# Eight modulation steps of the opening attention, and twelve of the first gather, cut into quarters and spread

## The chip, the cores and the metric

The kernel runs on one core of one Trainium2 chip. The metric is device time in microseconds (us) for one execution of the whole kernel; lower is better. Everything is in float32.

## The reference

Two transformer blocks with a shared residual stream `x` of 256 tokens by 1024 features. The first block has two layers with a second stream `ctx` of 256 tokens beside `x`; the second block has one layer. What matters here is the modulation: a small vector times a large matrix, whose six parts scale, shift and gate everything else.

```python
def _modulation(cvec, w_mod, b_mod):            # w_mod: 1024 x 6144 for each layer
    m = jax.nn.silu(cvec) @ w_mod + b_mod
    return jnp.split(m[:, None, :], 6, axis=-1)

for l in range(DEPTH):                           # DEPTH = 2
    m_x = _modulation(c, w_mod[l], b_mod[l])
    m_c = _modulation(c_ctx[None, :], w_mod[l], b_mod[l])
    h = _modulate(x, norm1_g[l], m_x[0], m_x[1])
    hc = _modulate(ctx, norm1_g[l], m_c[0], m_c[1])
    ...                                          # keys and values of ctx, attention, Fourier and pool branches
    x = x + m_x[2] * mix_x
    h2 = _modulate(x, norm2_g[l], m_x[3], m_x[4])
    x = x + m_x[5] * _peer(h2, w_pq[l], peer_keys[l], peer_down[l], peer_up[l])
```

`_peer` looks up, for each token, 128 rows of `peer_down` and 128 rows of `peer_up` (4 KB each), and is what most of the time goes to. The attention has 8 heads, 256 queries (two tiles of 128) and, in the part at hand, 512 keys.

## The kernel before

Each engine (TensorE, VectorE, ScalarE, GpSimd, SyncE) runs the same script, `main`, with its own subclass of `Walk`. A stage is a Python generator. Each `yield` ends a step, and the same step numbers hold on all five engines, since every subclass yields equally often. `self.run` plays one stage; `weave(front, back, rate, ...)` plays two at once: at every step of the front stage `rate` is added to an account, and while the account is at 1 or more a unit of the back stage is played and its cost (1.0, or what `at` says) is taken off. So the order on each engine's in-order queue is fixed when the program is built, by `rate`, by the costs and by the number of yields. Engines meet at semaphores, among them `full` and `free` of the eight PSUM banks (TensorE has written, the reader is done) and `w0` to `w2` (a weight buffer of 2 MB has landed).

The modulation of a layer is 12 steps j of `modvec`. One step is: SyncE loads a bias row and a 2 MB block of `w_mod` into a weight buffer; TensorE multiplies 8 times (2 columns by 512, the vector's columns stationary) into a bank; VectorE adds the bias; ScalarE stores 2 x 512 values to DRAM. SyncE starts a load into a buffer only when TensorE is through with what was in it (`fetch` waits for the mark `("w", ...)`, which the last of the eight products sets).

Two places use it inside a weave:

- The **beginning**. Steps 0 to 3 of layer 0 run by themselves. Steps 4 to 11 are the back stage of a weave whose front is `start1`: input projection (`tok_major`, 8 yields), queries, keys and values of the four token tiles (`qkv`, 6 + 6 + 3 + 3 yields), then `attend` (82 yields). The back has weight buffer 2 alone (slot "third"), the front buffers 0 and 1.
- The **first gather**, `weave(self.gather([0, 1, 2, 3], ...), ctx_then_x(queries), RATE0)` with 512 + 18 front steps, one for each looked-up row of a tile: GpSimd fetches a `peer_down` row and a `peer_up` row for each of 128 tokens, VectorE multiplies the former, TensorE sums the latter. `x_mix` plays the 12 steps of layer 1 in it, with buffers 0 and 1 by turns (slots "two").

In `attend` each head has two scores products (96 x 256), a maximum on VectorE, an exponential on ScalarE, four transposes on TensorE, a copy by VectorE (even heads) or ScalarE (odd heads), and four value products that wait for the copy. A head's values and the scores of the head two further on stand next to each other on TensorE.

Of the kernel before, what the change touches and what calls it, by code (L numbers as in the profile page):

```python
# [132 lines left out]
class Walk:  # L133
# [157 lines left out]
        pass  # L291

    def modvec(self, l, at, js):
        yield from self.units_of(len(js))

    def modsum(self, at, vectors):
        yield from self.units_of(4 * len(vectors) + 2)
# [126 lines left out]
    def main(self):  # L424

        K, A, NB = self.K, self.K.A, self.K.NB
# [6 lines left out]
        def temps(mem):  # L433
            return dict(qt=mem(768), kt=mem(768), kvt=mem(1024), junk=mem(256), rt=mem(3, 128), CQ=mem(2, 128), CK=mem(128))
# [7 lines left out]
        def att_bufs(mem):  # L442
            return [mem(512) for _ in range(2)], [mem(512) for _ in range(2)], mem(512)
# [6 lines left out]
        T0 = BG + 9216  # L450
# [10 lines left out]
        def mix_rest(l, who, HT, HP):  # L461
            self.small_weights(l)
            yield from self.at(1.0, self.spread(l, PL, FT, zpair(who), QT.rearrange("p (f c) n -> p f c n", c=2)[:, 0:2, :, :], QT[0:64, 4:8, :]))
            self.fence()
            mem = area((T0, NB))
            yield from self.at(1.5, self.gates(l, {0: AT, 1: FT, 2: PL}, QT, [mem(256) for _ in range(3)], mem(256), HT))
            self.fence()
            yield from self.at(3.4, self.project(l, who, QT, area((T0, NB))(512)))
            self.fence()
            yield from self.at(1.5, self.modulate(l, A["norm2_g"][l], 3, who, HP))  # L470
            self.fence()

        def start1():
            self.affine(K.arena[:, T0:T0 + 64], 0, HTx)
            self.affine(K.arena[:, T0:T0 + 64], 1, HTc)
            self.fence()
            for c0, n in ((0, 512), (512, 416)):
                yield from self.tok_major(0, c0, n, lambda i: K.H2[:, i, c0:c0 + n], (HTx, HTc))
            self.fence()
            self.small_weights(0)  # L480
            tm = temps(area((T0, NB)))
            for t in range(4):
                yield from self.qkv(0, t, zrow(t), tm, QT if t < 2 else None, (KTx, KTc)[t // 2], (VVx, VVc)[t // 2])
            self.small_done()
            self.fence()
            yield from self.attend(4, att_bufs(area((T0, NB))), QT, [(KTx, VVx), (KTc, VVc)], AT)
            self.fence()
# [22 lines left out]
        L1E = T0 + 4096  # L510

        def x_mix():
            yield from self.at(3.5, self.modvec(1, T0, range(12)))
            yield ("after", 2 * NEXT + LAG + 2)
            self.folded(2)
            self.fence()
            yield from self.at(1.5, self.modulate(1, A["norm1_g"][1], 0, 0, HTc))
            self.fence()
            for c0, n in ((0, 512), (512, 416)):
                yield from self.at(1.8, self.tok_major(1, c0, n, lambda i: K.H2[:, i, c0:c0 + n], (HTc,)))  # L520
            self.fence()
            self.small_weights(1)
            tm = temps(area((T0, NB)))
            for t in (0, 1):
                yield from self.at(1.4, self.qkv(1, t, zrow(t), tm, QT, KTc, VVc))
            self.fence()
            yield from self.spread(1, PL, FT, zpair(0), MX.rearrange("p (f c) n -> p f c n", c=2)[:, 0:2, :, :], MX[0:64, 4:8, :])
            self.fence()
            mem = area((L1E, NB))
            yield from self.at(1.6, self.gates(1, {1: FT, 2: PL}, MX, [mem(256) for _ in range(3)] + [ga], mem(256), HTc))  # L530

        def ctx_then_x(queries):
            yield from ctx_mix(queries)
            yield from x_mix()
# [14 lines left out]
        self.run(cols(2))  # L549
        self.run(cols(3))  # L550
        self.tables_there()
        self.weave(start1(), self.modvec(0, NB - 2048, range(4, 12)), 0.13, slots=("two", "third"))
        self.run(mix_rest(0, 0, HTx, HTp))
        self.slot, self.ring = self.slots["two"], self.rings["back"]
        queries = self.at(query_costs(3.2, 1.2, 0.7, 0.5), self.peer_q(0, 0, pt, HTp, QA))
# [1 line left out]
        self.weave(self.gather([0, 1, 2, 3], tables, gelu, [(0, 0, 5), (0, 0, 5), (0, 1, 5), (0, 1, 5)]),  # L557
                   ctx_then_x(queries), RATE0, done=done)
        self.folded(4)
# [142 lines left out]
class Vector(Walk):  # L702
# [76 lines left out]
    def modvec(self, l, at, js):  # L779
        K, S = self.K, self.S  # L780
        m = 2 if l < 2 else 1
        for j in js:
            bias, md = K.arena[0:m, at + 512 * (j % 2):at + 512 * (j % 2) + 512], K.arena[0:m, at + 1024 + 512 * (j % 2):at + 1536 + 512 * (j % 2)]
            b = self.bank()
            self.wait_ge(*self.full(b))
            self.wait_ge(*self.next(S.bias_in[j % 2], 16))
            stored = self.got.get(S.mod_out[j % 2].name, 0)
            if stored:
                self.wait_ge(S.mod_out[j % 2], stored)
            self.got[S.mod_out[j % 2].name] = stored + 16  # L790
            self.tt(md, b.ap[0:m, :], bias, AD, inc=self.drain(b))
            self.mark(("bias", l, j))
            yield
# [659 lines left out]
class Tensor(Walk):  # L1453
# [22 lines left out]
    def modvec(self, l, at, js):  # L1476
        K = self.K
        m, c0 = (2, 0) if l < 2 else (1, 2)
        for j in js:
            s = self.load()  # L1480
            w = s.ap.rearrange("p (k n) -> p k n", n=512)
            b = self.bank()
            self.wait_ge(*s.at)
            self.wait_ge(*self.vacant(b))
            for k in range(8):
                i = self.mm(b.ap[0:m, :], K.svb[:, k, c0:c0 + m], w[:, k, :], k == 0, k == 7)
            i.then_inc(*self.fill(b))
            self.rows_of[j] = b
            self.mark(("w", s.i, s.n))
            yield  # L1490
# [626 lines left out]
class Scalar(Walk):  # L2117
# [63 lines left out]
    def modvec(self, l, at, js):  # L2181
        K, S = self.K, self.S
        m = 2 if l < 2 else 1
        for j in js:
            md = K.arena[0:m, at + 1024 + 512 * (j % 2):at + 1536 + 512 * (j % 2)]
            b = self.bank()
            self.wait_ge(*self.drained(b))
            latest = self.latest
            self.e.dma_start(K.modd[2 * l:2 * l + m, 512 * j:512 * j + 512], md).then_inc(*self.inc(S.mod_out[j % 2], 16))
            self.latest = latest  # L2190
            yield
# [461 lines left out]
class Sync(Walk):  # L2653
# [17 lines left out]
    def modvec(self, l, at, js):  # L2671
        K, A, S = self.K, self.K.A, self.S
        m = 2 if l < 2 else 1
        src = A["w_mod"][l] if l < 2 else A["ada_w_2"][0]
        biases = A["b_mod"][l:l + 1, :] if l < 2 else A["ada_b_2"][0:1, :]
        if l:
            self.settled()
        for j in js:
            cs = slice(512 * j, 512 * j + 512)
            if j > 1:  # L2680
                self.wait_ge(*K.marks["bias", l, j - 2])
            self.e.dma_start(K.arena[0:m, at + 512 * (j % 2):at + 512 * (j % 2) + 512],
                             biases[0, cs].partition_broadcast(m)).then_inc(S.bias_in[j % 2], 16)
            self.fetch(self.load(), lambda a: a.rearrange("p (k n) -> p k n", n=512), src[:, cs].rearrange("(p k) n -> p k n", k=8))
            yield

    def tok_major(self, l, c0, n, dst, HTs):
        self.block(self.K.A["w_in"][l], c0, n)
# [80 lines left out]
        self.wait_ge(S.out, 32)  # L2769


RATE0 = 1.15
RATE1 = lambda s: 0.9 if s < 64 else 0.7 if s < 146 else 0.25
RATE2 = lambda s: 0.9 if s < 64 else 0.6
# [206 lines left out]
```

## Time and profile before

| | |
|---|---|
| median of 3 runs | 5015.89 us (5010.78 to 5027.59) |
| profiled execution | 5005.38 us, its span 5003.3 us |
| TensorE busy | 3628.7 us, 73% of the span |
| VectorE, GpSimd, ScalarE busy | 55%, 40%, 16% |
| DMA | 1328 MB, mean 265 GB/s |
| granted TensorE clock, mean | 0.807 of full speed |

The span is the time on the core from the first to the last instruction of the trace; the execution's own time is 2.1 us more. A TensorE product in float32 shows as two records, so eight products are "x16". The granted clock has two levels, 0.50 (1.2 GHz) and 1.00 (2.4 GHz); a value between is a stretch that had both.

### The profile page before, as it was taken

Reading aid. Unit: us, or ns where it says so; the run is one execution under the profiler, and the core shown is the slowest. Engines: PE = TensorE matmul, PEld = TensorE weight load, DVE = VectorE, ACT = ScalarE, POOL = GpSimd, SP = SyncE. Lnnn points to the kernel's source line nnn. Section 1 sums busy time; section 2 is a strip of 40 time slices with the busy share of each in tenths; the row PEclk is TensorE's granted clock in tenths of the full one; section 3 lists DMA queues with packets and bytes.
Section 4 is the critical chain, followed back from the end, with each engine's and each line's share of the span. In section 5 each row is a group of like instructions: output and inputs, shape, how many; then the busy total and the mean of one; then the engine's idle time right before and its main releaser. Section 6 shows DMA issues by size and latency. Waiting matters only on the chain.

```text
span 5003.3 us, 34906 instructions
## 1 busy us (share of the span) xinstructions
PE 3628.7 (73%) x10422; PEld 1830.2 (37%) x10422; DVE 2729.6 (55%) x5717; ACT 807.4 (16%) x1935; POOL 1992.1 (40%) x2088
## 2 busy tenths in 40 slices
PE   7679487877686676776564875676788886677776
PEld 3247343454342113541343421221366653332211
DVE  1211567454789646556545674576442222677676
ACT  1110112211121112111101111111121100111111
POOL 0000266554566543545102675475000000576775
PEclk9779799998776697986677998766778986899756
DMA  4234599999999998999436999898200002899999
GB/s 165 85 95 133 209 363 340 350 344 326 351 386 360 342 396 275 341 326 349 164 118 231 351 406 376 327 404 315 105 1 1 1 1 84 304 378 363 406 405 344
DMA packets 482032, 1328.11 MB, mean 265 GB/s; under 512 B 40396, under 2 KB 139980, under 8 KB 481336
## 3 DMA queue, kind: packets, MB, share of 16 engines
q0 software_dynamic: 301824, 1099.07, 57.9%
q1 hardware_dynamic: 173872, 204.09, 12.4%
q10 hardware_dynamic: 6152, 22.74, 1.3%
q8 instruction: 86, 1.41, 0.1%
q14 instruction: 98, 0.80, 0.0%
HBM read 1324.58 MB, written 1.17 MB: 265 GB/s over the span
## 4 chain that ended last, share of the span: by engine, by line
PE 24%; DMA 19%; DVE 8%; POOL 6%; issue 5%; ACT 2%; SPq 1%; ACTq 0%; DVEq 0%; POOLq 0%
PE ps L1458 23%; DMA arena<-in_peer_up,arena 7%; POOL arena L2649 6%; DMA arena<-in_peer_v,arena 4%; DVE arena L707 3%; DVE arena L720 3%; DMA arena<-in_w_mod 2%; ACT arena L2122 1%; DMA arena<-in_peer_down,arena 1%; DMA arena<-in_ada_w 1%; DMA arena<-in_peer_u,arena 1%; SPq L2661 1%; DMA arena<-in_w_oc 1%; PE ps L1464 1%; DMA arena<-mod_scratch 1%
## 5 line engine op out<-in xcount | busy, mean ns | idle before, releaser
L1458 PE MATMUL ps<-arena 128*128 128x512 f32 (+9 forms) x9844 | 3518.9, 511 | 1086.5 <-DMA arena<-in_peer_up,arena 330.7
L1458 PEld LDWEIGHTS ps<-arena 128*128 128x128 f32 (+4 forms) x9844 | 1739.3, 206 | 2808.5 <-issue 1382.6
L720 DVE SCALAR_TENSOR_TENSOR arena<-arena,ps 128x1024 f32<-128x1024 f32 x1024 | 1242.8, 1216 | 458.0 <-DMA arena<-in_peer_down,arena 284.0
L2649 POOL DMA_INDIRECT arena<-in_peer_down,arena x768 | 741.6, 966 | 1242.1 <-DVE arena L724 674.8
L2649 POOL DMA_INDIRECT arena<-in_peer_up,arena x768 | 735.0, 957 | 534.9 <-PE ps L1458 354.8
L2122 ACT ACTIVATE arena<-arena 128x128 f32<-128x128 f32 (+5 forms) x1250 | 446.9, 385 | 2152.2 <-PE ps L1458 975.2
L2649 POOL DMA_INDIRECT arena<-in_peer_u,arena x256 | 246.9, 964 | 896.5 <-DVE arena L724 804.1
L720 DVE SCALAR_TENSOR_TENSOR ps<-arena,ps 128x512 f32<-128x512 f32 x635 | 477.4, 752 | 121.3 <-DMA arena<-in_peer_up,arena 85.4
L707 DVE TENSOR_TENSOR arena<-ps,arena 128x512 f32<-128x512 f32 (+3 forms) x198 | 135.4, 684 | 563.8 <-PE ps L1458 533.2
L2122 ACT ACTIVATE arena<-ps 128x512 f32<-128x512 f32 (+3 forms) x345 | 175.1, 508 | 1198.9 <-PE ps L1458 885.9
L1464 PE MATMUL ps<-arena 128*128 128x128 f32 (+2 forms) x578 | 129.8, 372 | 282.0 <-DVE arena L707 194.9
L707 DVE TENSOR_TENSOR arena<-arena,ps 128x256 f32<-128x256 f32 (+2 forms) x136 | 74.4, 547 | 453.7 <-PE ps L1458 443.9
L2649 POOL DMA_INDIRECT arena<-in_peer_v,arena x256 | 243.8, 952 | 125.9 <-PE ps L1458 83.6
L707 DVE TENSOR_TENSOR arena<-arena 128x512 f32<-128x512 f32 (+9 forms) x412 | 252.1, 612 | 57.1 <-ACT arena L2122 38.6
L1464 PEld LDWEIGHTS ps<-arena 128*128 128x128 f32 (+2 forms) x578 | 94.2, 186 | 357.8 <-issue 183.3
L2122 ACT ACTIVATE arena<-ps,arena 128x256 f32<-128x256 f32 (+2 forms) x140 | 71.2, 509 | 712.7 <-PE ps L1458 441.6
L720 DVE SCALAR_TENSOR_TENSOR arena<-arena 128x512 f32<-128x512 f32 (+6 forms) x151 | 110.0, 729 | 63.2 <-DMA arena<-mod_scratch 56.1
L2122 ACT ACT_TABLE_LOAD x86 | 110.3, 1283 | 119.1 <-DVE arena L715 61.6
L724 DVE COPY arena<-ps 128x512 f32<-128x512 f32 (+5 forms) x69 | 39.6, 575 | 144.9 <-PE ps L1458 137.9
L728 DVE TENSOR_REDUCE arena<-ps 128x1 f32<-128x512 f32 (+2 forms) x50 | 30.3, 606 | 105.2 <-PE ps L1458 104.2
L1066 DVE MAX8 arena<-ps 128x8 f32<-128x128 f32 x128 | 28.7, 286 | 107.4 <-PE ps L1458 105.6
L720 DVE DVE_READ_ACCUMULATOR arena<-arena,ps 128x1 f32 x1024 | 83.6, 82 | 0.0
(33 smaller groups left out, 506.0 us busy)
## 6 DMA issues: line engine op xcount, KB each, us to landing
arena<-in_w_mod SPq DMA_DIRECT2D x24, 2048.0 KB, 13.5
arena<-in_w_in SPq DMA_DIRECT2D x72, 512.0 KB, 11.1
arena<-in_w_in SPq DMA_DIRECT2D x14, 2048.0 KB, 15.4
arena<-in_w_pq SPq DMA_DIRECT2D x12, 2048.0 KB, 10.0
arena<-in_ada_w POOLq DMA_DIRECT2D x24, 1024.0 KB, 7.4
arena<-in_w_out SPq DMA_DIRECT2D x8, 2048.0 KB, 11.4
arena<-mod_scratch ACTq DMA_DIRECT2D x26, 512.0 KB, 7.2
arena<-in_peer_down,arena POOLq DMA_INDIRECT x768, 6.9
```

The lines of the kernel that those rows point to most:

```text
L707: self.e.tensor_tensor(o, a, b, op).then_inc(*(inc or self.inc(self.S.vec)))
L720: self.e.scalar_tensor_tensor(o, a, s, b, op0, op1, accum_out=accum).then_inc(*(inc or self.inc(self.S.vec)))
L724: self.e.tensor_copy(o, a).then_inc(*(inc or self.inc(self.S.vec)))
L728: self.e.tensor_reduce(o, a, AX, op).then_inc(*(inc or self.inc(self.S.vec)))
L1066: e.max(v[j][:, 0:8], src[j]).then_inc(*self.inc(S.vec))
L1458: return self.e.matmul(o, l, r, start=start, stop=stop)
L1464: ins = self.e.transpose(o, x, self.K.ident)
L2122: self.e.activation(o, i, f, bias=bias, scale=scale, accum_out=accum).then_inc(*(inc or self.inc(self.S.act)))
L2649: self.e.indirect_dma_start(out=o, out_offset=None, in_=table, in_offset=bass.IndirectOffsetOnAxis(ap=idx.bitcast(U32), axis=0)).then_inc( ...
L2661: self.e.dma_start(f(s.ap), src).then_inc(self.S.w[s.i], 16)
```

## The change

`modvec` takes four yields for each j instead of one on every engine: TensorE issues two of its eight products in each, VectorE and ScalarE do their part in the fourth, SyncE issues the load in the first. In the beginning the rate 0.13 becomes 0.1 for the first 26 front steps and 0.45 after them; in the gather the cost 3.5 of a unit becomes 0.9.

```diff
     def modvec(self, l, at, js):
-        yield from self.units_of(len(js))
+        yield from self.units_of(4 * len(js))
...
         def x_mix():
-            yield from self.at(3.5, self.modvec(1, T0, range(12)))
+            yield from self.at(0.9, self.modvec(1, T0, range(12)))
...
-        self.weave(start1(), self.modvec(0, NB - 2048, range(4, 12)), 0.13, slots=("two", "third"))
+        self.weave(start1(), self.modvec(0, NB - 2048, range(4, 12)), lambda s: 0.1 if s < FIRST else 0.45, slots=("two", "third"))
...
             b = self.bank()
+            yield from self.units_of(3)
             self.wait_ge(*self.full(b))
...
             for k in range(8):
                 i = self.mm(b.ap[0:m, :], K.svb[:, k, c0:c0 + m], w[:, k, :], k == 0, k == 7)
+                if k % 2 == 1 and k < 7:
+                    yield
             i.then_inc(*self.fill(b))
...
             b = self.bank()
+            yield from self.units_of(3)
             self.wait_ge(*self.drained(b))
...
             self.fetch(self.load(), lambda a: a.rearrange("p (k n) -> p k n", n=512), src[:, cs].rearrange("(p k) n -> p k n", k=8))
-            yield
+            yield from self.units_of(4)
...
+FIRST = 26
```

By these numbers the units of the weave in the beginning stood behind front steps 8, 16, 24 (one each for j = 4, 5, 6) and 31, 39, 47, 54, 62 (j = 7 to 11). Now quarters of j = 4 stand behind steps 11, 21, 27 and 29, and the other 28 quarters two or three front steps apart from step 31 to step 91. The attention is steps 27 to 108.

TensorE's queue at the first heads of the attention, before. `2x512` is a product of `modvec`, `128x256` a scores product, `128x128` a transpose, `128x64` a value product; `w2` is the landing of the weight buffer.

```order
L1458 MATMUL ps<-arena 128x256 [waits free1]
L1458 MATMUL ps<-arena 128x256
L1458 MATMUL ps<-arena 2x512 [waits free7,w2]
L1458 MATMUL ps<-arena 2x512 x7
L1464 MATMUL ps<-arena 128x128 [waits free2,free0]
L1464 MATMUL ps<-arena 128x128 x3
L1458 MATMUL ps<-arena 128x64 [waits free2]
L1458 MATMUL ps<-arena 128x64 x3
L1458 MATMUL ps<-arena 128x256 x2
L1464 MATMUL ps<-arena 128x128 [waits free1]
L1464 MATMUL ps<-arena 128x128 x3
L1458 MATMUL ps<-arena 2x512 [waits free4,w2]
```

The same place now (all lines of the kernel behind line 781 have moved on by one or more):

```order
L1459 MATMUL ps<-arena 2x512 x4
L1459 MATMUL ps<-arena 128x256 [waits free1]
L1459 MATMUL ps<-arena 128x256
L1459 MATMUL ps<-arena 2x512 [waits w2]
L1459 MATMUL ps<-arena 2x512
L1465 MATMUL ps<-arena 128x128 [waits free2,free0]
L1465 MATMUL ps<-arena 128x128 x3
L1459 MATMUL ps<-arena 2x512 x2
L1459 MATMUL ps<-arena 128x64 [waits free2]
L1459 MATMUL ps<-arena 128x64 x3
L1459 MATMUL ps<-arena 128x256 x2
L1459 MATMUL ps<-arena 2x512 x2
```

The last four products of j = 4 and the first two of j = 5 now have one head's scores products between them, where a whole step had a head's work and more before the next; and a pair of products stands between a head's transposes and its value products.

TensorE's queue in the first gather, before. `128x512` with `up_in` is the sum of one looked-up row.

```order
L1458 MATMUL ps<-arena 2x512 [waits free5,w0]
L1458 MATMUL ps<-arena 2x512 x7
L1458 MATMUL ps<-arena 128x512 [waits up_in2,diagonal]
L1458 MATMUL ps<-arena 128x512 [waits up_in3,diagonal]
L1458 MATMUL ps<-arena 128x512 [waits up_in0,diagonal]
L1458 MATMUL ps<-arena 2x512 [waits free6,w1]
L1458 MATMUL ps<-arena 2x512 x7
```

And now:

```order
L1459 MATMUL ps<-arena 2x512 [waits free5,w0]
L1459 MATMUL ps<-arena 2x512
L1459 MATMUL ps<-arena 128x512 [waits up_in2,diagonal]
L1459 MATMUL ps<-arena 2x512 x2
L1459 MATMUL ps<-arena 128x512 [waits up_in3,diagonal]
L1459 MATMUL ps<-arena 2x512 x4
L1459 MATMUL ps<-arena 128x512 [waits up_in0,diagonal]
L1459 MATMUL ps<-arena 2x512 [waits free6,w1]
```

The eight products that stood in one block have a looked-up row's product between the pairs, and the number of rows for each modulation step is still three.

## Rows read from the trace of the kernel before

**Rows 1.** The page: the span, and DMA's busy tenths in 40 equal slices.

```profile
span 5003.3 us, 34906 instructions
...
DMA  4234599999999998999436999898200002899999
```

**Rows 2.** Stretches: length, TensorE busy (records), granted clock, DMA share, GB/s.

```profile
157.80:187.60 29.80, 20.00 (x47) 0.73 0.21 71
...
300.00:350.50 50.50, 39.35 (x136) 0.50 0.24 58
...
212.30:350.50 138.20, 103.97 (x344) 0.72 0.35 106
```

**Rows 3.** Timeline before the attention: start, us busy, what, [idle before, released by].

```profile
133.36 0.68 DVE L707 TENSOR_TENSOR arena<-ps,arena 2x512 f32<-2x512 f32 x1 [11.98 <-PE ps L1458]
...
136.57 0.66 PE L1464 MATMUL ps<-arena 128*128 128x128 f32 x2 [3.25 <-DVE arena L713]
...
146.59 1.94 PE L1464 MATMUL ps<-arena 128*96 128x128 f32 x8 [2.61 <-DVE arena L707]
...
157.84 0.69 PE L1464 MATMUL ps<-arena 128*128 128x128 f32 x2 [2.23 <-DVE arena L713]
...
187.60 0.48 PE L1464 MATMUL ps<-arena 128*128 128x128 f32 x1 [2.06 <-DVE arena L713]
...
197.90 0.48 PE L1464 MATMUL ps<-arena 128*128 128x128 f32 x1 [2.06 <-DVE arena L713]
```

**Rows 4.** Timeline of TensorE in the attention, same columns.

```profile
212.34 1.96 PE L1458 MATMUL ps<-arena 96*128 96x256 f32 x8 [1.22 <-ACT arena L2122]
215.14 7.04 PE L1458 MATMUL ps<-arena 128*2 128x512 f32 x16 [0.83 <-DMA arena<-in_w_mod]
222.11 0.66 PE L1464 MATMUL ps<-arena 128*128 128x128 f32 x4
223.74 2.02 PE L1458 MATMUL ps<-arena 128*128 128x64 f32 x12 [0.98 <-DVE arena L724]
...
230.93 10.95 PE L1458 MATMUL ps<-arena 128*2 128x512 f32 x28 [4.72 <-DMA arena<-in_w_mod]
...
248.82 8.59 PE L1458 MATMUL ps<-arena 128*2 128x512 f32 x16 [2.75 <-DMA arena<-in_w_mod]
...
266.12 10.42 PE L1458 MATMUL ps<-arena 128*2 128x512 f32 x28 [4.52 <-DMA arena<-in_w_mod]
...
284.65 9.44 PE L1458 MATMUL ps<-arena 128*2 128x512 f32 x16 [2.05 <-DMA arena<-in_w_mod]
...
295.65 1.10 PE L1458 MATMUL ps<-arena 128*128 128x64 f32 x8 [0.97 <-DVE arena L724]
...
300.02 1.11 PE L1464 MATMUL ps<-arena 128*128 128x128 f32 x4 [1.02 <-DVE arena L707]
...
318.32 3.78 PE L1458 MATMUL ps<-arena 128*128 128x64 f32 x12 [0.91 <-DVE arena L724]
321.90 1.06 PE L1464 MATMUL ps<-arena 128*128 128x128 f32 x4
```

**Rows 5.** Timeline of SyncE's queue: issue of the block for j = 8.

```profile
222.21 0.55 SPq L2661 DMA_DIRECT2D arena<-in_w_mod  x1
```

**Rows 6.** First gather: stretches (busy of PE, PEld, DVE, ACT, POOL; clock; DMA share; GB/s).

```profile
1712.00:1720.00 8.00, 7.44 (x16) 1.67 (x15) 2.40 (x4) 0.98 (x3) 0.32 (x1) 0.95 0.06 18
1720.00:1848.00 128.00, 102.62 (x217) 21.47 (x215) 58.60 (x99) 10.71 (x30) 56.04 (x60) 0.97 1.03 394
```

**Rows 7.** First gather, 1695 to 1848 us: who waited for whom (total, times, longest).

```profile
DVE arena L707 <- PE ps L1458: 84.0, 10, 22.4
POOL arena L2649 <- DVE arena L720: 74.1, 10, 22.0
PE ps L1458 <- DMA arena<-in_w_mod: 28.5, 8, 13.8
```

**Rows 8.** First gather: the twelve loads of `w_mod`, issue to landing.

```profile
DMA to landing us min/median/max: 12.3/18.2/19.8
```

## The prediction

> **What bounds the kernel now.** I read the page first: the span, and the DMA tenths. They split the kernel in two kinds of time: from slice 6 on, the gathers, with DMA at 9 tenths or more in most slices, and the first four slices (500 us), where DMA is busy 2 to 4 tenths and something else sets the pace [rows 1]. The change touches one place in each, so I went on with the timeline of TensorE in the beginning, the timeline of SyncE's queue for the landings, the stretches for the clock, and in the gather with the stretches and the table of waits.
>
> In the beginning TensorE's queue is the path. In the attention (212.3 to 350.5 us) it is busy for 104.0 of 138.2 us, and most idle pieces are of two kinds: it waits for a block of `w_mod` (five times, 0.83, 4.72, 2.75, 4.52 and 2.05 us, 14.9 in all) or about 1 us for a copy of transposed probabilities [rows 2, 4]. The load cannot be early. There is one buffer, so SyncE issues the next block when the last product on the old one is done: issued at 222.21, in use at 230.93, 8.7 us later; from the end of j = 9 at 257.41 to the start of j = 10 at 266.12 it is 8.7 us again [rows 4, 5]. So a wait is 8.7 us less the work that stands between one modulation step's last product and the next one's first. That is the sentence on which my forecast rests.
>
> The clock matters as well. The second tile's attention, without modulation work, ran at 0.50 throughout; a head there costs 3.78 + 1.06 us of TensorE against 2.02 + 0.66 at full clock [rows 2, 4].
>
> **The change part by part.**
>
> *Beginning, ahead of the attention.* Three whole steps go away from it and two quarters stay. (a) j = 4 stood behind the last input projection; VectorE's bias add at 133.36 came ahead of VectorE's fence, on which the next stage waits, so it goes in full: 7.0 us, the price of eight products at full clock [rows 3, 4]. (b) j = 5 stood in the second token tile, which took 187.60 - 157.84 = 29.8 us where the first took 21.3 without one: 8.5 us [rows 3]. (c) j = 6 stood in the fourth tile: 212.34 - 197.90 = 14.4 against 10.3 for the third, which has no fence behind it (1.2 us, the idle at 212.34): 5.3 us [rows 3, 4]. The first quarter now stands ahead of the wait of 2.61 us for the turned queries and costs nothing; if that cover were gone it would cost 1.7. The second stands in the third tile ahead of the keys' products, at low clock, where a pair is 3.5 us and about one of it lies in a wait that is there anyway: +2.4. Sum: -20.8 + 2.4 = **-18.4 us**; ends -13 (the tiles fall to 0.50 for longer, since the second tile's 0.73 owes something to its modulation products [rows 2]) and -21.
>
> *The attention, work.* A pair of products costs 7.04 / 4 = 1.76 us at full clock. 30 pairs now lie in the attention, 20 did. Heads cost, at full clock, 0.98 for scores, 1.04 for values and 0.63 for transposes, 16 of them 42.4 us [rows 4]. So the work is 42.4 + 52.8 = 95.2 us; it was 42.4 + 35.2 = 77.6.
>
> *The attention, waits for the block.* The order of the queue gives what stands in each of the seven gaps between j and j + 1, j = 4 to 10. One head's scores alone (1.0 us): wait 7.8. Values and scores, with the values held up some 2 us: ScalarE's copy has the store of modulation rows ahead of it in its queue, which waits for VectorE's bias add, which waits for the last pair; wait 3.9. Transposes alone (0.6), three times: 8.1 each. The end of the first tile (5.5 us from 295.65 to 301.13): 3.3. Transposes, a copy's wait, values and scores (3.6): 5.1 [rows 4]. Sum 44.4 us, where it was 14.9. This is the change's cost: a step's quarters stretch over some nine front steps and leave only two or three for the load, where a whole step left nearly eight.
>
> *The attention, other waits.* They were 138.2 - 104.0 - 14.9 = 19.3 us. A pair now stands between transposes and values in 11 of 16 heads and covers the copy, about 1.2 us each. Left: five heads, two tile ends of 2 us, and the held copy: 12 us.
>
> *The attention, clock.* Before, busy time above the price at full clock was 104.0 - 77.6 = 26.4 us. Four restarts after a wait cost 10.95 and 10.42 where 9.06 is due, 8.59 and 9.44 where 7.04 is: 1.8 us each on average [rows 4]. I take seven of them, 12.6, and 2.2 for each of three heads at low clock behind the last pair: 19 us. In between, pairs keep TensorE busy, so I take the high level for the second tile too, which is the change's gain here. Sum of the attention: 95.2 + 44.4 + 12 + 19 = 170.6 against 138.2: **+32.4 us**. Ends: +22 (all copies covered, restarts at 1.0) and +45 (restarts at 3.5).
>
> The Trainium skill speaks against this change. "TensorE: Matmul & The Clock Gate", section "HAM oscillation — how this bites in real kernels", says that where the products between two waits for a load last less long than the wait itself, the array falls back to half rate every time and each stretch starts cold. The work between waits is here some 12 us against waits of 3 to 8, so by that rule the clock would recover, and the trace agrees in the stretch from 230.93; the case in which it would not is a rival below.
>
> *What follows the attention.* The next stage's first weight block goes to the same buffer once j = 11 is done. That was at 294.1, 56 us before the attention's end; now it is some 20 us before it, since three to four heads are left [rows 2, 4]. A landing of 8.7 us still fits in twice: nothing. Without that cover it would be up to 8.7.
>
> *The first gather.* The cost 0.9 for a quarter makes 43.2 where 42 stood: all later units come one looked-up row later, and the number of rows is the same. The order there leaves three rows to a modulation step. From 1720 to 1848 DMA is full (share 1.03, 394 GB/s), and its bytes stay as they are, so finer pieces change nothing there [rows 6]. Ahead of it there is a hole: from 1712 to 1720 DMA is idle (share 0.06), since TensorE does the first eight products at a stretch, VectorE waits 22.4 us in its queue for them with its bias add, and GpSimd waits 22.0 for VectorE before it can fetch [rows 6, 7]. With quarters a looked-up row's product comes after two products, and VectorE's bias add three rows later, so the fetches go on earlier: of 8 us I take **-5**. Ends: -8 (the whole hole) and +5 (a row later at the end, or waits for `w_mod` grown by half a us each).
>
> *Sum.* -18.4 + 32.4 - 5 = **+9 us**, on the span 5012 (5003.3 before), on the profiled execution 5014. The median of the runs shown is 10.5 us above the profiled execution, so on it: 5015.9 + 9 = 5025; I say **5026**. That is +0.2%, within the 0.3% (15 us) that a measurement of this kernel can tell from no change, and near its edge.
>
> **The rivals.**
>
> *Slower at the gather: the blocks come later.* A load for j + 2 is issued at the end of j and needed at the start of j + 2. With 128 us for 11 steps, 11.6 each, that was 23.2 - 7.0 = 16.2 us, and is now 11.6 and what lies between two steps, about 2: 13.6. The landing takes 18.2 us in the median [rows 8], so TensorE's waits, 14.7 us besides the first [rows 7], would grow by up to 2.6 each, 29 in all: 5055. Against it: while TensorE waits, DMA works on just that block. It decides where DMA runs dry in those waits. Chance 0.12.
>
> *Slower in the attention: the clock stays low.* If the seven waits kept the clock down and every stretch runs at 0.50, as the second tile does [rows 2], heads cost 16 x 4.84 = 77, pairs 30 x 3.5 = 105, waits some 37, others 12: 231 against 138, +93 - 18 - 5: 5086. That is the case of the Trainium skill's section named above. Against it: 230.93 recovered within its row, 10.95 where twice 9.06 would be the low price [rows 4]. Chance 0.05.
>
> *Faster at the gather.* VectorE waits 84.0 us there for TensorE's modulation products and GpSimd 74.1 for VectorE [rows 7]. If those waits, and not DMA, set the pace, quarters would give back half of the 52 us that remain to GpSimd beyond the first: -26 more: 5000. Against it the full DMA [rows 6]. It decides only if DMA's share from 1720 on has holes that the mean hides. Chance 0.09.
>
> **How the numbers follow.** The forecast has 0.74, with a range of its own from 5013 to 5041: the ends of the terms do not all meet, and I take two thirds of their width, -12 and +15. That range holds both answers, with 5031 as the border: 0.50 for no difference and 0.24 for slower. With the rivals: faster 0.09, same 0.50, slower 0.24 + 0.12 + 0.05 = 0.41. The range that leaves out two in ten is 5008 to 5046; it holds nearly all of the forecast and the near half of two rivals.
>
> **What would show it.** In the profile after: TensorE reaches the first scores product at 194 us, not 212; seven waits for `w_mod` between it and the end of the attention, three of them near 8 us, 44 in all; the clock at 1.00 between them in the second tile; the end of the attention at 365 us, not 350; the hole in DMA's work before 1720 shorter by 5 us, and the gather's stretch otherwise as long as before. I am wrong if the waits for `w_mod` in the attention sum to less than 30 us (then it is faster or equal), if the clock stays at 0.50 between them (slower by far), or if the gather moves by more than 8 us either way.

## The result, and the profile after

| | before | changed |
|---|---|---|
| median of 18 runs | 5016.92 us | 5042.01 us |
| range of the runs | 4994.09 to 5046.28 | 5020.30 to 5070.60 |
| profiled execution's span | 5003.3 us | 5065.2 us |

The ratio is 1.0048, with a 95% interval of 1.0032 to 1.0064: 25 us slower (16 to 32). The profiled execution of the changed kernel is one of its longest, so I compare it by places and not by its end.

The timeline of TensorE in the attention of the changed kernel; columns as in [rows 4].

```profile
191.11 8.73 PE L1459 MATMUL ps<-arena 96*128 96x256 f32 x16 [1.22 <-ACT arena L2125]
207.75 3.48 PE L1459 MATMUL ps<-arena 128*2 128x512 f32 x4 [7.91 <-DMA arena<-in_w_mod]
...
228.50 5.06 PE L1459 MATMUL ps<-arena 128*2 128x512 f32 x8 [4.95 <-DMA arena<-in_w_mod]
...
248.27 7.42 PE L1459 MATMUL ps<-arena 128*2 128x512 f32 x20 [7.95 <-DMA arena<-in_w_mod]
...
270.38 11.63 PE L1459 MATMUL ps<-arena 128*2 128x512 f32 x24 [7.95 <-DMA arena<-in_w_mod]
...
293.38 10.79 PE L1459 MATMUL ps<-arena 128*2 128x512 f32 x24 [4.03 <-DMA arena<-in_w_mod]
...
334.36 7.09 PE L1459 MATMUL ps<-arena 128*2 128x512 f32 x20 [9.12 <-DMA arena<-in_w_mod]
...
341.96 5.65 PE L1459 MATMUL ps<-arena 128*2 128x512 f32 x20
...
369.84 6.16 PE L1459 MATMUL ps<-arena 128*128 128x256 f32 x16 [0.97 <-ACT arena L2125]
```

The attention begins at 191.1 us (212.3 before) and is over at 369.8 (350.5 before). The idle piece ahead of each modulation step's first pair grew to 4 to 9 us, and there are seven of them. The row at 341.96 is the good side: between two waits, pairs (two of a modulation step's eight products), values and scores stand without a gap, 20 records in 5.65 us.

The stretches of both attentions, from the first scores product to TensorE's first product behind the attention: length, TensorE busy (records), clock, DMA share, GB/s. Before:

```profile
212.34:350.50 138.16, 103.97 (x344) 0.72 0.35 106
```

Changed:

```profile
191.11:369.84 178.73, 119.99 (x385) 0.78 0.36 114
```

The clock is higher (0.78), the record count is that of ten more pairs, and yet the idle time rose from 34.2 to 58.7 us. The table of waits of that stretch says what ended it (total, times, longest):

```profile
PE ps L1459 <- DMA arena<-in_w_mod: 47.1, 7, 9.1
```

In the first gather, the stretch from the first of the twelve loads to the loads of the small weights: length; busy of PE, PEld, DVE, ACT and POOL; clock; DMA share; GB/s. Before:

```profile
1695.60:1917.50 221.90, 156.03 (x329) 39.62 (x330) 99.04 (x165) 24.33 (x63) 85.47 (x91) 0.88 0.94 356
```

Changed:

```profile
1719.30:1954.60 235.30, 165.17 (x331) 37.61 (x332) 100.92 (x168) 24.56 (x64) 87.38 (x93) 0.85 0.92 340
```

It is 13.4 us longer. Some 4 to 5 us of that are one more looked-up row that falls into it (93 GpSimd instructions against 91; two belong to a row, and 91 of them took 221.9 us). DMA's share fell from 0.94 to 0.92. The waits there, changed kernel, answer to [rows 7], though over the longer stretch; before it, TensorE's wait over that same stretch was 31.6 us:

```profile
DVE arena L707 <- PE ps L1459: 105.8, 12, 24.0
POOL arena L2653 <- DVE arena L720: 69.6, 16, 19.8
POOL arena L2653 <- PE ps L1459: 62.2, 25, 17.7
PE ps L1459 <- DMA arena<-in_w_mod: 45.4, 8, 17.0
```

GpSimd waits less for VectorE than before (112.3 us over the same stretch), and 62 us for TensorE, where it was 1.9.

What follows varies by itself. From the layer-1 keys' load to that of the second block's keys all eleven kernels of the first chips measured within 657.3 and 660.2 us. From there to the second block's output weights they took 1152.8 us (before), 1186.2 (changed), and 1159.8 to 1194.6 in the others, one execution each, with no order by what was changed; the one before is the shortest of the eleven. So the profiled pair's 62 us are 19 us up to the end of the attention, some 12 more by the layer-1 keys' load, and 33 us in that later stage, where the kernel before had a short draw and the changed one a long draw; some 3 us come back behind it. Of the 12, 4 lie between the attention and the gather, where the eleven kernels spread over 7 us; that leaves 7 or so for the gather.

### The profile page after: what moved, and what is told of

The parts are those of the page before. It is cut to its first block, busy times and chain, and to the rows that moved or that the text cites. A ratio compares the mean times of both kernels' runs of the same rounds, so it can differ in the third digit from the quotient of the medians.

```text
span 5065.2 us, 34911 instructions
## 1 busy us (share of the span) xinstructions
PE 3667.2 (72%) x10422; PEld 1841.7 (36%) x10422; DVE 2732.6 (54%) x5717; ACT 807.3 (16%) x1935; POOL 1982.4 (39%) x2088
## 3 DMA queue, kind: packets, MB, share of 16 engines
q1 hardware_dynamic: 173872, 204.09, 12.3%
## 4 chain that ended last, share of the span: by engine, by line
PE 41%; DMA 25%; DVE 17%; issue 6%; POOL 6%; ACT 3%; SPq 3%; ACTq 0%; DVEq 0%; POOLq 0%
PE ps L1459 39%; DMA arena<-in_peer_up,arena 9%; DVE arena L720 6%; POOL arena L2653 5%; DMA arena<-in_peer_v,arena 5%; DVE arena L707 5%; DMA arena<-in_w_mod 3%; SPq L2665 2%; ACT arena L2125 2%; DMA arena<-in_peer_down,arena 2%; DMA arena<-in_w_oc 2%; PE ps L1465 2%; DMA arena<-in_peer_u,arena 2%; DVE ps L720 2%; DMA arena<-in_ada_w 1%
## 5 line engine op out<-in xcount | busy, mean ns | idle before, releaser
L1459 PE MATMUL ps<-arena 128*128 128x512 f32 (+8 forms) x9844 | 3560.1, 515 | 1100.6 <-ACT arena L2125 314.5
L1459 PEld LDWEIGHTS ps<-arena 128*128 128x128 f32 (+3 forms) x9844 | 1754.3, 208 | 2844.2 <-issue 1430.4
## 6 DMA issues: line engine op xcount, KB each, us to landing
arena<-in_w_pq SPq DMA_DIRECT2D x12, 2048.0 KB, 10.5
```

The costliest lines, as they stand in the source:

```text
L1459: return self.e.matmul(o, l, r, start=start, stop=stop)
```

## The experiments

My theory (W): one weight buffer makes the load of the next block start at the last pair of this one, and quarters spread over some nine front steps leave the load only two or three; these waits are the loss. Rivals: the pairs themselves hold up the attention (P); the gather carries a good part of the loss (G); the steps' new places, and not the cut, are the loss (the run with an even rate, below).

Times of a kernel are medians; a ratio is to the kernel before on the same chips, with its 95% interval.

**Beginning alone.** The gather put back.

```diff
-            yield from self.at(0.9, self.modvec(1, T0, range(12)))
+            yield from self.at(3.5, self.modvec(1, T0, range(12)))
...
-            yield from self.units_of(3)
+            yield from self.units_of(PIECES[l] - 1)
...
+PIECES = (4, 1)
```

The places of `modvec` left out at the dots are changed in the same way: a step of layer l has `PIECES[l]` pieces.

> The changed kernel with the first gather put back: layer 1's modulation steps are whole again (one unit of cost 3.5), the beginning keeps its quarters and its rates. Theory W (the waits for w_mod in the opening attention are the loss, with one weight buffer the load starts when the last pair is done): those waits sum to about 47 us, the attention ends at about 370 us of the span (350 before), and the time is 19 us above the kernel before. Rival G (a good part of the 25 us comes from the gather): the beginning is the same, but what stands behind it must be level with the kernel before, so that the changed kernel is some 6 us slower than this one; if this one is as slow as the changed kernel, G falls.

Measured 5051.54 us against 5027.81, ratio 1.0042 (1.0022 to 1.0062): 21 us slower. Seven waits for `w_mod`, 47.5 us; the attention over at 372.6. That is the changed kernel's loss within what the two intervals can tell, so the beginning carries most of it.

**Gather alone.**

```diff
-            yield from self.at(3.5, self.modvec(1, T0, range(12)))
+            yield from self.at(0.9, self.modvec(1, T0, range(12)))
...
+PIECES = (1, 4)
```

> The kernel before with only the first gather changed: layer 1's modulation steps in quarters of cost 0.9, the beginning whole at rate 0.13. Theory W: the attention ends at 350 us, and the time is within 5 us of the kernel before. Rival G: 6 us or more slower, to be seen between the first w_mod load of the gather and the loads of the next attention's small weights. My forecast had said 5 us faster there.

Measured 5020.74 us, ratio 1.0003 (0.9979 to 1.0028): no difference in the time, though the interval has room for 14 us. The attention was over at 351.5. The place itself can be read closer than the whole: from the gather's first `w_mod` load to the layer-1 keys' load it took 679.4 us here, 671.0 before.

**Quarters with two buffers.** The changed kernel, steps 4 to 11 in buffers 2 and 1 by turns.

```diff
-SLOTS = {"three": [0, 1, 2], "two": [0, 1], "third": [2]}
+SLOTS = {"three": [0, 1, 2], "two": [0, 1], "third": [2], "pair": [2, 1]}
...
-        self.weave(start1(), self.modvec(0, NB - 2048, range(4, 12)), lambda s: 0.1 if s < FIRST else 0.45, slots=("two", "third"))
+        self.weave(start1(), self.modvec(0, NB - 2048, range(4, 12)), lambda s: 0.1 if s < FIRST else 0.45, slots=("two", "pair"))
```

> The changed kernel with one edit: the modulation steps 4 to 11 of the beginning use weight buffers 2 and 1 by turns instead of 2 alone (buffer 1 is not used by the front stage once its input projection is done), so a block's load can start a whole step earlier. Theory W: a load has some 20 us, its waits go to about 0 in the attention, the clock stays at the high level, and the attention takes 95 us of work, some 12 of other waits and about 11 of low clock: 118 us, ends near 310 us of the span, 60 us sooner than in the changed kernel; time near 4982. Rival P (pairs between the attention's steps hold up the copies and maxima behind them in the queues, and the waits for w_mod only stand where the others would): the attention stays above 150 us, and the time above 5010.

Measured 4990.93 us, ratio 0.993 (0.9903 to 0.9957): 35 us below the kernel before. The timeline of TensorE, with the attention's first row, the copy's wait at 211.70, three rows of pairs that now begin without a wait for a load, and the first row behind the attention:

```profile
190.87 10.54 PE L1459 MATMUL ps<-arena 96*128 96x256 f32 x20 [1.21 <-ACT arena L2125]
...
211.70 5.55 PE L1459 MATMUL ps<-arena 128*128 128x64 f32 x20 [1.74 <-ACT arena L2125]
...
217.78 5.64 PE L1459 MATMUL ps<-arena 128*2 128x512 f32 x20
...
236.27 1.88 PE L1459 MATMUL ps<-arena 128*2 128x512 f32 x4
238.35 5.55 PE L1459 MATMUL ps<-arena 128*128 128x64 f32 x20 [0.20 <-ACT arena L2125]
...
308.60 5.93 PE L1459 MATMUL ps<-arena 128*128 128x256 f32 x16 [0.97 <-ACT arena L2125]
```

And its stretch:

```profile
190.87:308.60 117.73, 105.94 (x385) 0.89 0.50 155
```

No wait for `w_mod` is left, the attention takes 117.7 us where 118 was expected, and the clock is 0.89. The one edit took 61 us out of the same order of products, 47 us of waits and 14 us of busy time: the second is the low clock behind each wait. P falls (it wanted an attention above 150 us and a time above 5010): with its load out of the way the cut order is no burden, and the missing buffer is where the time went. The wait of 1.74 us at 211.70 is ScalarE's copy behind the store of a modulation row, with all loads out of the way.

**Whole steps with two buffers.** The same `SLOTS` edit on the kernel before.

> The kernel before with the same two buffers for its whole modulation steps. Theory W: the 14.9 us of waits for w_mod go, and some 7 us of low clock behind them: the attention takes 116 to 120 us instead of 138, time some 20 us below the kernel before. With rival P the quarters would be worse than whole steps once loads are out of the way, so this kernel would beat the changed one with two buffers by 20 us or more; with W the two are within 25 us and the quarters are the faster, by the three steps that they took out of the stage ahead of the attention at no cost to a full TensorE queue.

Measured 4994.67 us, ratio 0.994 (0.9918 to 0.9962). Its attention:

```profile
215.12:330.50 115.38, 96.10 (x344) 0.76 0.38 113
```

The 14.9 us of waits and 7.9 us of busy time are gone, as expected. Here too no wait for `w_mod` stands in the attention. It is over at 330.5, so in the profiled executions quarters and their new places, taken together, are worth 21.9 us at the end of the attention once the load has room. The whole times, 4990.93 against 4994.67 us, don't show it: the quarters in the gather take 11 us of it back (681.1 us from the first `w_mod` load to the keys' load, 670.2 with whole steps), and the rest is within what they can tell.

**Quarters with two buffers, gather whole.** The two edits together: `"pair"` and `PIECES = (4, 1)` with cost 3.5.

> The changed kernel's beginning with weight buffers 2 and 1 by turns, and the first gather's modulation steps whole again (cost 3.5). If the two places are independent: the attention ends at 308 to 309 us as with quarters and two buffers, the time from the gather's first w_mod load to the keys' load of layer 1 is 670 us as in every kernel with whole steps so far (669, 670, 671), not 680 as in every one with quarters (678, 679, 681). Time some 10 us below the kernel with two buffers and quarters in both places: about 4981 where the kernel before has 5028, 47 below it. If the 10 us in the gather were chance, it is level with that kernel.

Measured 4978.41 us against 5027.33, ratio 0.9896 (0.9865 to 0.9927): 49 us below the kernel before, the lowest median of all. Its interval still overlaps those of the two kernels above (0.9903 to 0.9957, and 0.9918 to 0.9962 for whole steps), so that it beats them is likely and not shown by the times. The attention was over at 309.6, the gather's stretch took 674.3 us.

**A pause for the load, one buffer.**

```diff
-        self.weave(start1(), self.modvec(0, NB - 2048, range(4, 12)), lambda s: 0.1 if s < FIRST else 0.45, slots=("two", "third"))
+        self.weave(start1(), self.at(8 * [1.0, 1.0, 1.0, 7.0], self.modvec(0, NB - 2048, range(4, 12))), lambda s: 0.1 if s < FIRST else 1.0, slots=("two", "third"))
```

The edit is shown against the changed kernel's beginning; the gather is whole.

> One buffer in the beginning as in the changed kernel, quarters too, but their costs are 1, 1, 1 and 7 at a rate of 1 in the attention: four quarters behind four front steps in a row, then a pause of seven steps for the load. The gather is whole. By the rule of my forecast (wait = 8.7 us less the work between a step's last product and the next one's first): transposes, a copy's wait, values, scores and transposes lie in the gap, 4.4 us, so each of seven waits is some 4.3 us, 30 in all instead of 47. Fewer copies are covered, 17 us of other waits; attention 157 us, from 191 to 348, 22 us sooner than in the changed kernel; time level with the kernel before or up to 5 us below it. If the waits do not follow the gap, they stay above 40 us and the attention ends at 360 or later.

Measured 5027.47 us, ratio 1.0008 (0.9987 to 1.0028), no difference. Three of the seven waits:

```profile
205.08 11.26 PE L1459 MATMUL ps<-arena 128*2 128x512 f32 x28 [4.21 <-DMA arena<-in_w_mod]
225.04 13.14 PE L1459 MATMUL ps<-arena 128*2 128x512 f32 x28 [4.50 <-DMA arena<-in_w_mod]
247.77 10.46 PE L1459 MATMUL ps<-arena 128*2 128x512 f32 x28 [5.39 <-DMA arena<-in_w_mod]
```

All seven make 31.1 us, 30 expected: the waits do follow the gap in the order. The end missed, 359.3 for 348. Its attention has 166.5 us with 118.1 busy, so other waits are 17.3 as expected, and the low clock is what I had too small, by about 8 us. These waits are shorter than the changed kernel's (2.8 to 5.4 us), and yet what follows them costs no less: a row of 28 records, 9.06 us at full clock by the prediction's price, took 10.46 to 13.14 us in six cases.

**The cut without the move, one buffer.**

```diff
-        self.weave(start1(), self.modvec(0, NB - 2048, range(4, 12)), lambda s: 0.1 if s < FIRST else 0.45, slots=("two", "third"))
+        self.weave(start1(), self.modvec(0, NB - 2048, range(4, 12)), 0.52, slots=("two", "third"))
```

Again against the changed kernel's beginning, with a whole gather.

> The beginning in quarters but not moved: an even rate of 0.52 in the place of 0.1 and 0.45, so the modulation steps lie over the same front steps as before the change (2 to 62), each cut in four. One buffer, the gather whole. This is the cut without the move. The waits in the attention should be five of 6 to 8 us, 32 in all (14.9 before, 47 in the changed kernel), since the gap between steps is two front steps here as well; the attention's end 355 to 365 us. If the move and not the cut were the loss, it ends at 350 or sooner.

One run, 5024.11 us against one of 5014.82 before: the attention from 218.5 to 365.8 us, its end just beyond the 365 that I had expected at most. Of its waits for `w_mod`, one:

```profile
234.44 11.67 PE L1459 MATMUL ps<-arena 128*2 128x512 f32 x24 [7.84 <-DMA arena<-in_w_mod]
```

Five in the attention, 35.7 us, and two of 2.3 us ahead of it. It ends 15 us later than before the change without anything moved. So in this one run the cut, spread over the steps, is enough for most of the loss at that mark (19 us in the changed kernel). The move in the changed kernel took 21 us out of the stage ahead and brought the same work and two more waits into the attention.

**Quarters in the idle pieces ahead of the attention too.** Two buffers, gather whole, rates 0.3 and 0.38.

> As the kernel with two buffers and a whole gather, but with rates 0.3 and 0.38: seven quarters ahead of the attention instead of two, to lie in the idle pieces of 2 to 3 us of the queries and keys. Five pairs less in the attention, 9 us; two of them now cost their full 1.8 us ahead of it and three little. The attention ends at 303 to 309 us; time within 5 us of that kernel, rather below it. It tells whether those idle pieces are free room, as the quarter at 146 us suggested.

Measured 4988.93 us, ratio 0.992 (0.9891 to 0.9949), 10.5 us above the kernel with rates 0.1 and 0.45 where I had expected 5 at most, rather below; the intervals overlap, so neither is shown to be faster. The attention ran from 196.4 to 307.6: its end comes 2.0 us sooner than there, so the room is small.

**The gather: squeezed quarters, and the one row.** With whole steps and cost 3.5 the stretch from the first `w_mod` load to the layer-1 keys' load was 669.2 to 676.7 us in seven kernels (mean 672.5), with quarters of 0.9 it was 678.4, 679.4 and 681.1 (mean 679.6). First I squeezed the quarters.

```diff
-            yield from self.at(0.9, self.modvec(1, T0, range(12)))
+            yield from self.at(12 * [0.2, 0.2, 0.2, 3.0], self.modvec(1, T0, range(12)))
```

> The kernel before with the first gather's modulation steps in quarters, but with costs 0.2, 0.2, 0.2 and 3.0 instead of 0.9 four times: the four quarters fall in one front step or two, and a pause of nearly three follows, so that a block's load has nearly the time that it had with whole steps. Theory L (quarters spread over three rows leave the load less time, TensorE's waits for it grow, and DMA runs dry at the end of them): the stretch to the keys' load falls back from 679 to 670 us, the waits for w_mod besides the first from 26 us to about 15. Rival Q (the cut itself costs, through VectorE's bias add that stands in another place): it stays at 679.

One run (5057.74 us, against a median of 5027.33 before). TensorE's waits for `w_mod` fell to 33.2 us in seven, 15.0 of it the first (42.5 with quarters of 0.9), and the stretch stayed at 677.2. Theory L, that the waits are the loss in the gather, does not hold up. But the costs summed to 43.2 here as well, and I had not taken that out. So: quarters with the old sum, whole steps with the new one, and squeezed quarters with the old one.

```diff
-            yield from self.at(0.9, ...        # quarters, sum 43.2
+            yield from self.at(0.875, ...      # quarters, sum 42
...
-            yield from self.at(3.5, ...        # whole, sum 42
+            yield from self.at(3.6, ...        # whole, sum 43.2
```

> The kernel before with the first gather's modulation steps in quarters of cost 0.875, so that twelve steps cost 42 as before the change, and every later unit keeps its looked-up row (with 0.9 they cost 43.2 and all later units come one row later). Measured is the stretch from the gather's first w_mod load to the keys' load of layer 1: 669 to 677 us with whole steps in seven kernels, 678 to 681 with quarters of 0.9 in three. If the cut is the loss: 679 again. If the one row is: 672. The shorter stretch to the loads of the small weights holds 4 us for the one row itself: 235 with it, so 231 without it if the cut costs the rest.

> The kernel before with the cost of a whole modulation step in the first gather raised from 3.5 to 3.6: nothing is cut, but twelve steps cost 43.2 and all later units come one looked-up row later, as with the change. If the one row is the loss: the stretch to the keys' load is 679 us. If the cut is: 672, as with whole steps so far.

> As the kernel with the squeezed quarters, but with costs 0.2, 0.2, 0.2 and 2.9, 42 for the twelve steps. That kernel had the waits for w_mod nearly back to those of whole steps, and yet a stretch of 677 us. If the one row is what was left of the loss, 672 here; if the cut itself costs by VectorE's bias add in another place, 677 again.

These three ran on a slower chip (the kernel before took 5165.61 us there), and no kernel with whole steps of 3.5 was profiled on it, so the 672 and 679 us that I had expected don't apply, and only the three compare with each other.

| one run each | stretch to the keys' load | to the small weights | waits for `w_mod` |
|---|---|---|---|
| quarters, sum 42 | 683.3 us | 224.0 us | 40.1 us |
| squeezed, sum 42 | 684.4 us | 225.0 us | 29.3 us |
| whole, sum 43.2 | 688.2 us | 232.2 us | 28.7 us |

The two with the cut aren't the longer ones, and the one with the longest waits for blocks is the shortest of the three; the kernel in which nothing was cut and all is one row later is the longest, by 4 to 5 us. On the shorter stretch all fourteen kernels agree: 232.2 to 236.3 us in the five with the sum 43.2, 221.9 to 229.7 in the nine with 42, cut or not, of which 4 to 5 us is the one row itself. That points to the row and away from the cut. It isn't settled: each is one run, kernels of the same order are up to 7.5 us apart in the stretch to the keys' load, and the stage behind it, which is the same in all three, took 674.5 to 679.1 us on this chip, 4.6 us apart as well.

## Why the prediction was right, and where it was not

The change made the kernel 25 us slower (16 to 32), I had said 9. The sign is right and 5042 us lie in my range of 5008 to 5046, though near its end and just outside the forecast's own 5013 to 5041; half of my chances had been on no difference. The mechanism was right: the waits for the block are the cost, and they came as the order of the queue gave them. Three terms were off, and with what the profiled executions show in their place (-21.2, +40.6, and +7 by the means of the stretches) the sum is 26 us. That the number fell inside all the same is owed to the width of the range, which had been made for the rivals.

*The base, a wait is 8.7 us less the work in the gap.* Right. I had 7.8, 3.9, 8.1, 8.1, 3.3, 5.1 and 8.1 us from the order alone; measured were 7.91, 4.95, 7.95, 7.95, 4.03, 5.25 and 9.12, 47.1 for 44.4. The last is the odd one: there 9.8 us passed from the last product on the old block to the first on the new. The kernel with a pause and the one with two buffers bear the rule out from both sides.

*Ahead of the attention, -18.4.* Measured -21.2. The three steps taken out gave 7.4, 7.7 and 6.1; the first quarter did better than nothing: the row of the turned queries waits 0.81 us instead of 2.61 and the tile is 2.0 us shorter, as its clock was high for longer (0.77 where it was 0.66). The second quarter cost 1.6 us for 2.4. I had the clock only as a risk.

*The attention, +32.4.* Measured +40.6, the term that was mis-sized. Other waits were 11.6 us for 12. Busy time was 120.0 us: 95.2 at full price, and 24.8 for the low clock, where I had 19. The kernel with two buffers has the same products without the waits, so it can be set beside this one row by row. The seven restarts cost 1.7, 1.5, 1.8, 4.2, 1.4, 1.9 and 1.4 us, 14.0 for my 12.6. They don't follow the length of the wait: the longest, 9.12 us, cost 1.4, and of two waits of 7.95 us one cost 1.8 and the other 4.2. That was at 270.38, where products that took 1.88 and 5.55 us without the wait (236.27 and 238.35) took 11.63; the granted clock stayed at 0.50 until 279.3, 8.9 us into work without a gap. Why this one was so long is open. The larger part of the miss stands in the kernel with two buffers too, where busy time is 10.7 us above the full price and I had 6.6 (the last three heads, which did cost some 6.5). What I had left out is the start of the attention. The first row, scores of two heads and two pairs, is 5.5 us at full price and took 8.73, with the clock at 0.50 until 197; before the change a whole modulation step stood just ahead of the attention, and its first row ran at 1.00 (1.96 us for the scores at 212.34). Where a pair stands just ahead, in the kernel with rates 0.3 and 0.38, the first row of 20 records took 7.50 us, and 10.54 in the two-buffer kernel without one.

The section of the Trainium skill that I cited, "TensorE: Matmul & The Clock Gate", "HAM oscillation — how this bites in real kernels", says of its kernel that each wait lets the clock fall and the next stretch starts cold. The trace agrees: the clock was 0.50 in the first 2 us behind each of the seven waits. It was back at 1.00 ahead of each next wait, so the rival with a low clock throughout did not come.

*The gather, -5.* Wrong in sign: +7 by the means of the stretches. I expected DMA's idle hole before the first row to shrink. It changed its form: idle for some 5 us and then half busy for some more, about 6.5 us of DMA's time missing where it had been 7.6. And TensorE was done with the first block later: the next load of that buffer was issued 28.3 us after the first load, where it had been 23.0; 3 us of that are a longer wait for the first landing (17.0 us for 13.8). My rival "the blocks come later" saw its waits come (45.4 us for 31.6), but those waits don't seem to be what costs: squeezed quarters had 33.2 us of them for 42.5 and stayed long. What my sum had at nothing is the row by which all later units come later; it was only in the upper end of the term, +5. The runs point there, but don't settle it, and why one row should cost more than itself is open. The term moved by 7.3 us in the profiled pair and 8.3 in the kernel with the gather alone, the edge of the 8 us that I had named as a sign of being wrong.

*What follows the attention, nothing.* Right: the stage behind began 19.9 us later (387.02 for 367.13), the attention ended 19.3 later.

## What to carry to other kernels

Before work that waits for a buffer is cut fine and spread, subtract: the time a reload takes from the last use to the next first use, less what the order leaves between those two. Spreading the use of a single buffer takes that time away from its reload, however well the pieces fill other gaps. Give the load its own room first, by a second buffer that the other stage has done with; here that alone was worth 30 us for whole pieces (19 to 41 by the interval; 20 us at the end of the attention). Only with it did the fine cut bring the end of the attention forward, by a further 21.9 us; that the whole kernel gains by the cut as well is likely and not shown. And count what the moved work did for the stage that it left: here it had kept the clock up at the attention's start (3.3 us).

## What the runs showed of the hardware

A wait costs twice. With the same products in the same order, 47 us less of waiting for loads brought 14 us less of busy time (119.99 to 105.94 us), with a granted clock of 0.89 in place of 0.78. Among these waits the second price does not go by their length: row by row it was 1.4 to 4.2 us for each of seven waits of 4.0 to 9.1 us, and 1.4 to 4.1 us for six waits of 2.8 to 5.4 us in the kernel with a pause. A wait of 0.83 us cost nothing more in the kernel before: the row behind it, at 215.14, is at full price [rows 4].

A 2 MB block took 8.5 to 9.6 us from issue to landing while little else was loaded (median 8.8, in the changed kernel's attention), and 12.3 to 19.8 (median 18.2) beside the gather's fetches at 394 GB/s [rows 6, 8].

An execution's length can move in a stage that nobody touched: 1152.8 to 1194.6 us between two marks of the second block over eleven kernels, where the 658 us ahead of it repeat within 3 (657.3 to 660.2). The 18 runs of the kernel before spread over 52 us as a whole. So a change of 10 us is read from marks around its place, over several kernels, and not from the whole time of one execution.
